# A streaming encoder layer on one core: 64-row attention scores in two row halves, and a new order of each attention step

## The reference

```python
z = rmsnorm(h, g_mix) @ w_in                     # q | k | v | u | g_a | g_b
s = einsum('bnqkgd,bnskd->bnkgqs', q, k) * HEAD_DIM ** -0.5
s = s - alibi_slopes * dist
s = where(valid, s, MASK_VALUE)                  # chunk mask, window of 2 chunks
probs = softmax(concatenate([s, sink]))[..., :-1]   # one learned sink per head
a = einsum('bnkgqs,bnskd->bnqkgd', probs, v)
d = pool_mix(u)                                  # means over 2/4/8/16 frames minus the frame
m = sigmoid(g_a) * (a @ w_branch_a) + sigmoid(g_b) * (b @ w_branch_b)
h += m @ w_out;  h += relu(rmsnorm(h) @ w_up)**2 @ w_down;  h += gate * e
```

## Time and profile before

| | us |
|---|---|
| median of 3 runs | 1683.36 (1682.65 to 1683.42) |
| profiled execution | 1683.38 |
| its span | 1681.6 |
| TensorE matmuls busy | 1659.2 |
| VectorE busy | 853.3 |
| ScalarE busy | 669.9 |
| GpSimd busy | 83.8 |

### The profile page before, as it was taken

How to read it: one execution, slowest core, us unless ns; L and a number is a source line. 1 busy time by engine, 2 the same in 40 slices (tenths; PEclk the granted TensorE clock), 3 DMA queues, 4 the chain that set the end, 5 groups by cost and what they waited for, 6 DMA issues and landing times.

```text
span 1681.6 us, 29214 instructions
## 1 busy us (share of the span) xinstructions
PE 1659.2 (99%) x11298; PEld 1650.8 (98%) x11298; DVE 853.3 (51%) x1179; ACT 669.9 (40%) x972; POOL 83.8 (5%) x76
## 2 busy tenths in 40 slices
PE   7999999999999999999999999999999999999997
PEld 7999999999999999999999999999999999999997
DVE  7577544444445556443344443344433544565765
ACT  6355534333333444443234433334333344444442
POOL 3034000000000003000000000000000300000000
PEclk9999999999999999999999999999999999999998
DMA  7533544444444444444444444444444444444431
GB/s 283 171 118 126 196 149 150 148 149 150 149 150 158 150 150 151 150 150 150 150 150 150 149 147 148 147 151 147 147 148 147 149 148 150 148 149 150 151 125 62
DMA packets 37961, 252.48 MB, mean 150 GB/s; under 512 B 5281, under 2 KB 6689, under 8 KB 8481
## 3 DMA queue, kind: packets, MB, share of 16 engines
q1 hardware_dynamic: 35136, 245.59, 41.1%
q10 hardware_dynamic: 2784, 6.35, 1.0%
HBM read 248.65 MB, written 3.27 MB: 150 GB/s over the span
## 4 chain that ended last, share of the span: by engine, by line
PE 97%; DVE 2%; ACT 0%; DMA 0%; issue 0%; POOL 0%; DVEq 0%; SPq 0%; POOLq 0%; ACTq 0%
PE acc L404 32%; PE acc L405 32%; PE acc L406 32%; PE s_ps L456 1%; DVE w_lo L811 0%; DMA h<-in_x 0%; PE o_ps L434 0%; PE t_ps L443 0%; DVE h L1162 0%; DVE sumsq L876 0%; ACT xa_hi L602 0%; DVE xa_lo L867 0%; ACT w_hi L581 0%; POOL prob_t L343 0%; PE m_ps L418 0%
## 5 line engine op out<-in xcount | busy, mean ns | idle before, releaser
L581 ACT ACTIVATE w_hi<-raw 128x1024 fp32r<-128x1024 f32 x462 | 487.4, 1059 | 882.5 <-PE acc L406 878.9
L404 PE MATMUL acc<-xa_hi,w_hi 128*128 128x320 f32 x2112 | 655.6, 310 | 9.1 <-DVE xa_lo L867 9.1
L405 PE MATMUL acc<-xa_lo,w_hi 128*128 128x320 f32 x2112 | 653.6, 309 | 0.0
L406 PE MATMUL acc<-xa_hi,w_lo 128*128 128x320 f32 x2112 | 653.6, 309 | 0.0
L811 DVE TENSOR_TENSOR w_lo<-raw,w_hi 128x1024 fp32r<-128x1024 f32 x462 | 550.5, 1232 | 19.3 <-ACT w_hi L581 19.0
L404 PEld LDWEIGHTS acc<-xa_hi,w_hi 128*128 128x128 f32 x2112 | 397.5, 188 | 9.9 <-DVE w_lo L811 9.3
L405 PEld LDWEIGHTS acc<-xa_lo,w_hi 128*128 128x128 f32 x2112 | 397.5, 188 | 0.2
L406 PEld LDWEIGHTS acc<-xa_hi,w_lo 128*128 128x128 f32 x2112 | 397.4, 188 | 0.0
L404 PE MATMUL acc<-xb_hi,w_hi 128*128 128x320 f32 x1280 | 395.8, 309 | 0.0
L405 PE MATMUL acc<-xb_lo,w_hi 128*128 128x320 f32 x1280 | 395.5, 309 | 0.0
L406 PE MATMUL acc<-xb_hi,w_lo 128*128 128x320 f32 x1280 | 395.5, 309 | 0.0
(11 more groups left out here) (161 smaller groups left out, 943.6 us busy)
## 6 DMA issues: line engine op xcount, KB each, us to landing
raw<-in_weights SPq DMA_DIRECT2D x229, 1024.0 KB, 4.8
h<-in_x SPq DMA_DIRECT2D x4, 640.0 KB, 8.0
h<-in_x ACTq DMA_DIRECT2D x1, 2560.0 KB, 12.8
raw<-in_weights SPq DMA_DIRECT2D x4, 512.0 KB, 9.2
out_y<-h ACTq DMA_DIRECT2D x2, 800.0 KB, 3.5
bias<-in_alibi SPq DMA_DIRECT2D x1, 512.0 KB, 11.3
out_y<-h ACTq DMA_DIRECT2D x1, 480.0 KB, 2.6
p_raw<-in_p_in ACTq DMA_DIRECT2D x1, 320.0 KB, 2.8
```

Source lines behind the costliest of these rows:

```text
L404: nc.tensor.matmul(out, w_hi[:, at:at + P], x_hi[:, m * T:(m + 1) * T], start=k == 0, stop=False)
L405: nc.tensor.matmul(out, w_hi[:, at:at + P], x_lo[:, m * T:(m + 1) * T], start=False, stop=False)
L406: mm = nc.tensor.matmul(out, w_lo[:, at:at + P], x_hi[:, m * T:(m + 1) * T], start=False, stop=k == depth - 1)
L581: nc.scalar.activation(w_hi[:, dst:dst + HALF], raw[:, src:src + HALF], ACT.Copy).then_inc(hi_done, 1)
```

## The change

Queries are no longer padded: `q` holds one chunk of queries in 128 rows, side 0 (one key/value head) in rows 0 to 63 and side 1 in rows 64 to 127, and two neighbouring query chunks side by side in the 128 columns. A score matmul takes 64 rows of `q` and `kx`; side 0 writes bank `s_ps`, side 1 bank `m_ps`, which are now one tensor of two banks. The rows of the scores are therefore other heads than before, and the bias and the sinks are brought into that layout: the bias by eight DMAs, the sinks by four and by four small GpSimd copies. The clearing of `q` goes. The scaling with the bias reads both banks. In each step the order on TensorE becomes transposes, scores, product with v; on ScalarE copy of the transposes, exponentials, a_hi; on VectorE reciprocal, scores, a_lo.

```diff
-                q = sb("q", 2 * KA * T, F32, earlier)
+                q = sb("q", KA * T, F32, earlier)
...
-        s_ps, t_ps, o_ps, m_ps = psum("s_ps"), psum("t_ps"), psum("o_ps"), psum("m_ps")
+        sm_ps = ctx.enter_context(nc.psum_tensor("sm_ps", [P, 2 * 512], F32))
+        s_ps, m_ps = sm_ps[:, 0:512], sm_ps[:, 512:1024]
+        scores = (s_ps, m_ps)
+        t_ps, o_ps = psum("t_ps"), psum("o_ps")
...
-            for dst, src in ((pscale, post_scale), (sink, sinks), (icnt, inv_count), (ident, ident_in),
-                             (hst, hist), (bias, alibi)):
+            for dst, src in ((pscale, post_scale), (icnt, inv_count), (ident, ident_in), (hst, hist)):
                 nc.sync.dma_start(dst[:, :], src).then_inc(const_in, 16)
             load(3, 3)
+            for n in range(4 * NPAIR):
+                p, side, odd = n // 4, n // 2 % 2, n % 2
+                to, of = (slice(h * CHUNK, (h + 1) * CHUNK) for h in (odd, side))
+                at, half = p * QPP, QPP // 2
+                nc.sync.dma_start(
+                    bias[to, (at + side * half) * KEYS:(at + (side + 1) * half) * KEYS].rearrange(
+                        "t (c k) -> t c k", c=half),
+                    alibi[of, at * KEYS:(at + QPP) * KEYS].rearrange(
+                        "t (c o k) -> t c o k", c=half, o=2)[:, :, odd, :]).then_inc(const_in, 16)
+            for n in range(4):
+                side, odd = divmod(n, 2)
+                to, of = (slice(h * CHUNK, (h + 1) * CHUNK) for h in (odd, side))
+                nc.sync.dma_start(sink_in[to, side * KA:(side + 1) * KA], sinks[of, :]).then_inc(const_in, 16)
...
-            nc.gpsimd.memset(q[:, :], 0.0).then_inc(q_zero, 1)
+            pool.wait_ge(xodd, KD // 2 + 1)
+            pool.wait_ge(const_in, CONSTS)
+            for n in range(4):
+                if n:
+                    pool.wait_ge(sink_done, n)
+                side, odd = divmod(n, 2)
+                rows = slice(odd * CHUNK, (odd + 1) * CHUNK)
+                nc.gpsimd.tensor_copy(
+                    sink[rows, :].rearrange("t (p s c) -> t p s c", p=NPAIR, s=2)[:, :, side, :],
+                    sink_in[rows, side * KA:(side + 1) * KA].rearrange("t (p c o) -> t p c o", p=NPAIR, o=2)[:, :, :, odd]
+                ).then_inc(sink_done, 1)
...
-                    for c in range(QPP):
-                        qc = ((p * QPP + c) * NB + b) * P
-                        mm = nc.tensor.matmul(s_ps[:, c * KEYS:(c + 1) * KEYS], q[:, qc:qc + P],
-                                              kx[:, kc:kc + KEYS], start=True, stop=True)
+                    for c in range(QPP // 2):
+                        qc = ((p * QPP // 2 + c) * NB + b) * P
+                        for side in range(2):
+                            rows = slice(side * HD, (side + 1) * HD)
+                            mm = nc.tensor.matmul(scores[side][:, c * KEYS:(c + 1) * KEYS], q[rows, qc:qc + P],
+                                                  kx[rows, kc:kc + KEYS], start=True, stop=True)
                     mm.then_inc(at_qk, 1)
+                if 0 <= i - 3 < NG:
+                    g = i - 3
...
-                for side in range(2):
-                    rows = slice(side * HD, (side + 1) * HD)
-                    ins = nc.vector.tensor_tensor(
-                        q[rows, at:at + 2 * T].rearrange("p (b s t) -> p b s t", b=NB, s=2)[:, :, side, :],
...
+                nc.vector.tensor_tensor(
+                    q[:, two * 2 * T:(two + 1) * 2 * T].rearrange("p (b o t) -> p b o t", b=NB, o=2)[:, :, odd, :],
+                    acc[u % BANKS][:, 0:T].rearrange("p (b t) -> p b t", b=NB),
+                    r[:, :].rearrange("p (b t) -> p b t", b=NB), ALU.mult).then_inc(taken, 1)
...
                     nc.vector.scalar_tensor_tensor(
-                        out=pg, in0=s_ps[:, :], scalar=HD ** -0.5,
-                        in1=bias[:, p * QPP * KEYS:(p + 1) * QPP * KEYS], op0=ALU.mult, op1=ALU.add).then_inc(at_s, 1)
+                        out=pg.rearrange("p (s k) -> p s k", s=2),
+                        in0=sm_ps[:, :].rearrange("p (s k) -> p s k", s=2)[:, :, 0:QPP // 2 * KEYS],
+                        scalar=HD ** -0.5,
+                        in1=bias[:, p * QPP * KEYS:(p + 1) * QPP * KEYS].rearrange("p (s k) -> p s k", s=2),
+                        op0=ALU.mult, op1=ALU.add).then_inc(at_s, 1)
```

More of the change, by code:

```diff
@@ L214, in encoder_step @@
         pscale = sb("pscale", KA)
-        sink = sb("sink", KA)
+        sink, sink_in = sb("sink", KA), sb("sink_in", 2 * KA)
         def gain(g, c):
@@ L262, in encoder_step @@
         v_tr, v_copy = sem("v_tr"), sem("v_copy")
-        q_zero = sem("q_zero")
+        sink_done = sem("sink_done")
         line_a = sem("line_a")
@@ L293, in encoder_step @@
         yv = sem("yv")
-        CONSTS = 16 * 6
+        CONSTS = 16 * (8 + 4 * NPAIR)
         block = ctx.enter_context(nc.Block())
@@ L350, in probabilities @@
                 nc.gpsimd.tensor_tensor(pg, pg, of, ALU.mult).then_inc(at_p, 1)
+            pool.wait_ge(sink_done, 4)
             for g in range(U_U - U_STEP - 1):
@@ L453, in step @@
                     kc = p * KX + window(b)
-                    for c in range(QPP):
-                        qc = ((p * QPP + c) * NB + b) * P
-                        mm = nc.tensor.matmul(s_ps[:, c * KEYS:(c + 1) * KEYS], q[:, qc:qc + P],
-                                              kx[:, kc:kc + KEYS], start=True, stop=True)
-                    mm.then_inc(at_qk, 1)
+                    for c in range(QPP // 2):
[4 more added lines that the diff above has]
+                                                  kx[rows, kc:kc + KEYS], start=True, stop=True)
+                    mm.then_inc(at_qk, 1)
+                if 0 <= i - 3 < NG:
+                    g = i - 3
+                    b, p = GROUPS[g]
+                    pe.wait_ge(at_tc, g + 1)
+                    if g:
+                        pe.wait_ge(at_l, g)
+                    src = prob_t[:, (g % 2) * QPP * P:(g % 2 + 1) * QPP * P].rearrange(
+                        "k (s c t) -> k s c t", s=2, c=QPP)
+                    for side in range(2):
+                        at = (b * NPAIR + p) * P + side * HD
+                        out = o_ps[side * HD:(side + 1) * HD, 0:QPP * CHUNK].rearrange("d (c t) -> d c t", c=QPP)
+                        mm = nc.tensor.matmul(out, vt[:, at:at + HD], src[:, side, :, :], start=True, stop=True)
+                    mm.then_inc(at_o, 1)
             for u in range(U_KV, U_STEP):
@@ L633, in step @@
             def step(i):
[L634 to L641, removed]
                 if 0 <= i - 2 < NG:
@@ L657, in step @@
                     nc.scalar.activation(es[:, mine], es[:, mine], ACT.Exp).then_inc(at_e, 1)
+                if 0 <= i - 3 < NG:
+                    g = i - 3
+                    b, p = GROUPS[g]
+                    act.wait_ge(at_o, g + 1)
+                    dst = a_hi[:, :].rearrange("p (c t) -> p c t", c=KA)[:, p * QPP:(p + 1) * QPP,
+                                                                         b * CHUNK:(b + 1) * CHUNK]
+                    nc.scalar.activation(dst, o_ps[:, 0:QPP * CHUNK].rearrange("p (c t) -> p c t", c=QPP),
+                                         ACT.Copy).then_inc(at_h, 1)
             def pool_high(c):
@@ L900, in queries @@
                 dve.wait_ge(used, 2 * u + 2)
-                at = (u - U_Q) * 2 * T
-                for side in range(2):
-                    rows = slice(side * HD, (side + 1) * HD)
-                    ins = nc.vector.tensor_tensor(
-                        q[rows, at:at + 2 * T].rearrange("p (b s t) -> p b s t", b=NB, s=2)[:, :, side, :],
-                        acc[u % BANKS][rows, 0:T].rearrange("p (b t) -> p b t", b=NB),
-                        r[rows, :].rearrange("p (b t) -> p b t", b=NB), ALU.mult)
-                ins.then_inc(taken, 1)
+                two, odd = divmod(u - U_Q, 2)
+                nc.vector.tensor_tensor(
+                    q[:, two * 2 * T:(two + 1) * 2 * T].rearrange("p (b o t) -> p b o t", b=NB, o=2)[:, :, odd, :],
+                    acc[u % BANKS][:, 0:T].rearrange("p (b t) -> p b t", b=NB),
+                    r[:, :].rearrange("p (b t) -> p b t", b=NB), ALU.mult).then_inc(taken, 1)
                 ahead(u, u)
-            dve.wait_ge(q_zero, 1)
             for u in range(U_Q, U_STEP):
@@ L923, in step @@
             def step(i):
[L924 to L932, removed]
                 if 0 <= i - 1 < NG:
@@ L957, in step @@
                                             ALU.add).then_inc(at_m, 1)
+                if 0 <= i - 3 < NG:
+                    g = i - 3
+                    b, p = GROUPS[g]
+                    dve.wait_ge(at_h, g + 1)
+                    rows, cols = slice(p * QPP, (p + 1) * QPP), slice(b * CHUNK, (b + 1) * CHUNK)
+                    nc.vector.tensor_tensor(a_lo[:, :].rearrange("p (c t) -> p c t", c=KA)[:, rows, cols],
```

(4 more changed lines are left out.)

## The result

| | before | after |
|---|---|---|
| median, us | 1682.68 (7 runs) | 1688.86 (7 runs, 1688.52 to 1689.10) |
| ratio to before, 95% interval | | 1.0035 [1.0025, 1.0045] |
| span of the profiled execution, us | 1681.6 | 1687.2 |
| TensorE matmuls busy, us | 1659.2 | 1659.4 |
| VectorE busy, us | 853.3 | 851.5 |

The change makes the kernel slower by 0.35%, 5.9 us by the ratio. The prediction was 1688.5 us, 5.1 us over the profiled execution of before. No engine has more work to speak of: ScalarE's busy time went from 669.9 to 670.8 us, VectorE's fell.

The account below looks back on a forecast made before the run. TensorE bounds the kernel before; VectorE and ScalarE were to bound the pooling passes, four of them 1.00 us longer each, outweighing TensorE's early saving: shift +5.08, 1683.38 + 5.1 = 1688.5 us, range 1680.5 to 1690.5.

Parts of the forecast that it names:

- The bound changes hands: Pooling passes: VectorE and ScalarE become the bound at about 10.1 us a pass, and TensorE stands at the product.
- a_lo's wait: VectorE's step: a_lo, now last, waits for ScalarE's a_hi copy behind four exponentials; VectorE idle about 2 us, steps 3 to 9.
- M: Start of a step's first exponential on ScalarE; VectorE was free at about M before, forecast at M + 2.37 after.
- The doubling over the pooling product: GpSimd's first doubling lies over pool_mean's small product L972 in every pass, making it take 0.74 us, not 0.17.
- rival 2: Pooling passes: the loop binds but GpSimd's doubling doesn't lie over L972; 4 x 0.57 us less, 1686.2 us; chance 0.12.
- The row halves run together: Score matmuls on TensorE: eight records on two row halves take 0.445 us, not 0.89.
- Rival 3: Score matmuls: the row halves run one after the other, 0.89 us of scores; 1690.3 us; chance 0.10.
- the five slots: Score matmuls: if matmuls start in program order, eight records need five slots, not four; 0.4 us over the forecast.
- The change of the array's division: TensorE's attention steps: each entry to or exit from a division of the array costs about 0.15 us.
- From VectorE's end to the next evacuation: After the last pooling pass: step 10's product starts 0.04 later, takes 0.58, unit 7.04, evacuation 0.04 later.
- Parts costed at nothing: Query and scores evacuation, GpSimd's clearing and sink copies, SP's queue of loads: taken as 0, the queue bounded -0.4 to +0.5 us.
- the 2.5 us that I gave TensorE for itself: Attention steps: TensorE saves 0.145 us in steps 0 to 2 and 0.295 in steps 3 to 9, if nothing else moved.

Follow-up runs that it names:

- the run without the first doubling: The changed kernel with GpSimd's first doubling of each chunk replaced by a memset that reads nothing; 1684.64 us, ratio 1.0011 to before.
- a_hi first: The changed kernel with ScalarE's a_hi copy back at the start of its step, VectorE's a_lo still last; 1681.22 us, ratio 0.9991 to before.
- both blocks first: The changed kernel with a_hi first on ScalarE and a_lo first on VectorE, only TensorE keeping the new order; 1681.71 us, ratio 0.9994 to before.
- before with two exponentials: The kernel before with two of the four exponentials of each group left out on ScalarE; 1682.95 us, ratio 1.0002 to before.
- the kernel with the sides in turn: The changed kernel with score matmuls issued both of side 0, then both of side 1; 1688.65 us, ratio 1.0036 to before.

## Why the prediction was right, point by point

The mechanism was right, and the forecast of 1688.5 us stands 0.4 us from the median of 1688.86. That this is so close is in part luck: the shift was forecast as 5.1 us and measured as 5.9 by the ratio, 6.2 by the medians and 5.80 at 180 us of the trace. The forecast was made against 1683.38 for one execution, and the seven runs of before have a median of 1682.68; that 0.7 us hides much of the miss.

- **The bound changes hands.** Right, and shown from four sides: the two waits are there, only kernels with a_hi behind the exponentials lose, cutting exponentials helps only there, and four passes of the loop are as long as forecast (40.41 us, forecast 36.44 + 4.00). TensorE's waits at the product were forecast as 1 to 1.5 us each and were 0.17 to 1.88.
- **a_lo's wait.** By the sum a_lo starts at M + 1.65 + 0.36 + 0.03 = M + 2.04; measured 171.49 - 169.45 = 2.04 (the wait itself, from the end of es, is 2.08). VectorE is free at M + 2.37; measured 171.84 - 169.45 = 2.39.
- **The doubling over the pooling product.** Right in every pass, 0.74 us. Its price was right too: the four last passes are 2.30 us shorter without it, and rival 2 had 4 x 0.57 = 2.3. The 4.04 us of the run without the first doubling is more because it also frees the three places in which before has the same overlap.
- **The row halves run together.** Right: four slots of 0.11. Rival 3 falls, and so do the five slots that the prediction named beside its sum.
- **The change of the array's division.** The mis-sized term. I took 0.15 us for each from the column halves. A step with scores alone costs 85.80 - 77.92 - 7.04 = 0.84 us, so two changes cost 0.84 - 0.445 = 0.40, 0.20 each; the full step's three cost 8.90 - 7.04 - 1.32 = 0.54 (8.90 from the kernel with a_hi first). Steps 0 to 3 saved 0.35 us and not 0.73: 110.89 - 77.92 = 32.97 against 111.35 - 78.03 = 33.32. That the first scores of after stood 0.11 us earlier hides some of it, so that 0.27 of it are in the 0.72 us by which the trace (5.80) passes my 5.08.
- **From VectorE's end to the next evacuation.** The other 0.45. I had 0.04 + 0.58 + 7.04 + 0.04 = 7.70; measured 179.99 - 171.84 = 8.15. Two things are in it. I counted 0.58 for the product "with its exit", but that row holds only the entry: the way back to the full array comes on top and makes the first matmul of the unit 0.35 long on the chain and not 0.15. It does so behind a product that did not wait as well (0.34 at 103.66). That is 0.20. The rest, 0.26, is the standstill: the product starts at 172.07, 0.23 behind VectorE's next start and not 0.04, and takes 0.65 and not 0.58.
- **Parts costed at nothing.** Right. The eight bias issues on SP's queue took 9.03 us and the four of the sinks 2.52, and the fifth weight load went out at about 21.3 us where before had 13.93; it cost nothing, for the first attention step stood at 77.92 against 78.03.

Three kernels come out at or under before: the row halves in the old order, both blocks first, and a_hi first, which is the fastest measured here, 1681.22 us, 0.09% under before and at the edge of what can be told from no change. Of the 2.5 us that I gave TensorE for itself, 1.5 are there; the dearer changes of division take 0.3 in steps 0 to 2, 0.1 in each of the seven full steps, and 0.05 at step 10.

## What to carry to other kernels

In a step that several engines share, look not only at what an instruction costs but at what it now stands behind: a copy of 0.36 us moved behind four exponentials lengthened a loop between two engines that are idle for a fifth and for nearly half of a pass of before, and made it the bound of a third. Before moving a block to the tail of a step on every engine, follow who waits for it in the next step, and move it on the engine where the wait pays only. And where GpSimd and VectorE share a stretch, small shifts of start decide which operation is held up; whether that costs anything is decided by whether VectorE is in the bounding loop (0.57 us a pass in after, nothing in before with two exponentials).

## What was not expected

**A fall of TensorE's clock that cost nothing.** In the profiled execution of after, TensorE stood for 1.88 us at 131.65, and from 133.2 us on its matmuls started 0.27 us apart and not 0.147, until 136.5; the granted clock of the stretch says the same. Windows of after (stretch, length, PE, PEld, DVE, ACT, POOL, clock, DMA share, GB/s), and under them the same of the kernel with the sides in turn, whose TensorE had stood for 1.86 us in the same place:

```profile
130.00:134.00 4.00, 2.35 (x14) 1.99 (x15) 2.88 (x8) 3.94 (x13) 1.58 (x2) 0.90 0.01 4
134.00:138.00 4.00, 4.00 (x21) 4.00 (x21) 3.94 (x6) 0.28 (x1) 3.21 (x3) 0.67 0.26 33
```
```profile
134.00:138.00 4.00, 4.00 (x30) 4.00 (x29) 3.97 (x6) 0.33 (x1) 3.21 (x3) 1.00 0.22 33
```

One fell to the lower of its two levels (1.2 GHz) for a while, the other kept 2.4 GHz. The next wait of TensorE for a_lo took the loss up:

```profile
142.33 0.65 PE L485 MATMUL o_ps<-prob_t,vt 128*64 128x256 f32 x4 [0.17 <-DVE a_lo L981]
```

In the kernel with the sides in turn the same wait was 1.71 us, and both kernels reached 172.1 us together. It is also why the waits of TensorE sum to 5.5 us in after and to 7.0 in the other, and why TensorE is busy for 1659.4 us in after and for 1657.5 in the other. An estimate from the two waits: had TensorE been the bound there, the fall would have cost 1.71 - 0.17 = 1.5 us. It is one case of each; why one fell and the other not stays open.

**The price of a division depends on what follows.** Into column halves it is 0.15 us (0.58 - 0.43), and from column halves to the transposes 0.15 (0.59 - 0.44, rows 3). From column halves back to a unit it is 0.20, in both kernels: the first matmul of the unit takes 0.34 to 0.35 on the chain and not 0.15. The chain of before in step 12, and of after in step 3, behind the product:

```profile
183.84 0.35 PE acc L404
```
```profile
103.66 0.34 PE acc L430
```

So this price stood in the trace of before, in a row that I had not looked at. From row halves to a unit it is 0.20 too, and from row halves to column halves 0.15. Only the way from the full array into the row halves is dearer than its like with column halves: 0.65 - 0.445 = 0.20. Inside it, the first pair of records stands alone for 0.21 us where the later ones are 0.11 apart. Why it is dearer was not tried.
